# Two transformer blocks on one core: squares of the first norm between the conditioning slabs, norm roots by logarithm and exponential, low parts on VectorE, weights split late

## What is computed

```python
def rms_norm(x, g, eps):
    return x * lax.rsqrt(jnp.mean(x * x, -1, keepdims=True) + eps) * g

mod = silu(c) @ w_ada[l] + b_ada[l]            # shift, scale, gate, two times
a_x = rms_norm(h_x, g_mix[l]) * (1 + sc1) + sh1   # norm mix, tokens
a_c = rms_norm(h_c, g_mix[l]) * (1 + csc1) + csh1 # the same for the context rows
y_x, y_c = mixer(a_x, a_c, w_in[l], ...)       # projections, a Fourier mix, two attentions
h_x = h_x + gt1 * y_x
f_x = rms_norm(h_x, g_ffn[l]) * (1 + sc2) + sh2   # norm ffn
h_x = h_x + gt2 * conv_ffn(f_x, ...)
```

## Time and profile before

| what | us |
|---|---|
| runs (3) | 2770.31, 2776.19, 2776.48 |
| median | 2776.19 |
| profiled execution, its own time | 2759.57 |
| its span, first to last instruction | 2757.8 |
| TensorE matmul busy | 2562.5 (93%) |
| VectorE busy | 1576.3 (57%) |
| ScalarE busy | 1219.8 (44%) |
| POOL busy | 187.4 (7%) |
| mean granted TensorE clock | 0.974 |

### The profile page before, as it was taken

The page is one execution under the profiler, slowest core; times in us unless marked ns, Lnnn a source line. Parts: engine busy times, 40 slices in busy tenths (PEclk is TensorE's granted clock), DMA queues, the critical chain, the costliest instruction groups (busy, mean ns, idle before and its releaser), DMA issues.

```text
span 2757.8 us, 42208 instructions
## 1 busy us (share of the span) xinstructions
PE 2562.5 (93%) x17840; PEld 2259.0 (82%) x17840; DVE 1576.3 (57%) x2657; ACT 1219.8 (44%) x2025; POOL 187.4 (7%) x239
## 2 busy tenths in 40 slices
PE   5997899998999998999989989999799999988999
PEld 2875577776777776878889989998799999976999
DVE  2333234545565555364668877666566675766665
ACT  3224334424333324354556554445444553555543
POOL 0000000000000000000000011010010110025100
PEclk8998999999999999999999999999899999999999
DMA  7224432231454543233354546554265456530554
GB/s 243 67 86 131 134 105 84 67 99 61 136 169 138 168 131 129 85 115 101 122 168 155 190 145 207 185 168 130 71 201 190 153 191 199 168 126 16 169 197 140
DMA packets 337387, 382.12 MB, mean 139 GB/s; under 512 B 7408, under 2 KB 301296, under 8 KB 337200
## 3 DMA queue, kind: packets, MB, share of 16 engines
q1 hardware_dynamic: 334656, 370.37, 41.2%
q0 software_dynamic: 2544, 9.06, 1.1%
HBM read 378.36 MB, written 1.05 MB: 138 GB/s over the span
## 4 chain that ended last, share of the span: by engine, by line
PE 77%; DVE 10%; ACT 8%; DMA 3%; issue 2%; POOL 0%; SPq 0%; DVEq 0%; ACTq 0%; POOLq 0%
PE PS L1207 20%; PE PS L1209 19%; PE PS L1208 19%; DVE WL L1899 3%; ACT WH L1579 2%; PE PS L1242 1%; PE PS L1244 1%; PE PS L1243 1%; PE PS L1255 1%; PE PS L1224 1%; DMA RAWB<-in_w_in 1%; PE PS L1225 1%; PE PS L1226 1%; PE PS L1273 1%; PE PS L1340 1%
## 5 line engine op out<-in xcount | busy, mean ns | idle before, releaser
L1899 DVE TENSOR_TENSOR WL<-RAWB,WH 128x1024 fp32r<-128x1024 f32 (+2 forms) x613 | 734.7, 1206 | 650.5 <-ACT WH L1579 649.0
L1207 PE MATMUL PS<-AH,WH 128*128 128x256 f32 (+1 forms) x2912 | 910.7, 313 | 13.8 <-DVE WL L1899 13.8
L1209 PE MATMUL PS<-AH,WL 128*128 128x256 f32 (+1 forms) x2912 | 896.6, 308 | 0.0
L1208 PE MATMUL PS<-AL,WH 128*128 128x256 f32 (+1 forms) x2912 | 896.5, 308 | 0.0
L1579 ACT ACTIVATE WH<-RAWB 128x1024 fp32r<-128x1024 f32 (+2 forms) x613 | 625.3, 1033 | 320.0 <-PE PS L1209 167.1
L1207 PEld LDWEIGHTS PS<-AH,WH 128*128 128x128 f32 x2912 | 548.9, 189 | 70.1 <-issue 22.1
L1209 PEld LDWEIGHTS PS<-AH,WL 128*128 128x128 f32 x2912 | 548.7, 188 | 31.1
L1208 PEld LDWEIGHTS PS<-AL,WH 128*128 128x128 f32 x2912 | 548.5, 188 | 29.6 <-issue 0.5
L1207 PE MATMUL PS<-BH,WH 128*128 128x256 f32 (+1 forms) x1440 | 452.2, 314 | 0.8 <-DVE WL L1899 0.8
L1209 PE MATMUL PS<-BH,WL 128*128 128x256 f32 (+1 forms) x1440 | 439.2, 305 | 0.0
L1208 PE MATMUL PS<-BL,WH 128*128 128x256 f32 (+1 forms) x1440 | 438.5, 305 | 0.0
(11 more groups left out here) (314 smaller groups left out, 2827.9 us busy)
## 6 DMA issues: line engine op xcount, KB each, us to landing
RAWB<-in_f_in SPq DMA_DIRECT2D x88, 1024.0 KB, 5.2
RAWB<-in_w_in SPq DMA_DIRECT2D x52, 1024.0 KB, 5.1
RAWB<-in_w_ada SPq DMA_DIRECT2D x48, 1024.0 KB, 5.4
RAWB<-in_w_up SPq DMA_DIRECT2D x44, 1024.0 KB, 5.2
RAWB<-in_f_out SPq DMA_DIRECT2D x40, 1024.0 KB, 5.1
RAWB<-in_w_down SPq DMA_DIRECT2D x20, 1024.0 KB, 5.3
RAWB<-in_sb_qkv SPq DMA_DIRECT2D x12, 1024.0 KB, 5.4
RAWB<-in_w_out SPq DMA_DIRECT2D x8, 1024.0 KB, 5.1
```

The source lines that it names most:

```text
L1207: pe.matmul(out, h, xh[:, 0:T], start=k == 0, stop=False)
L1208: pe.matmul(out, h, xl[:, 0:T], start=False, stop=False)
L1209: i = pe.matmul(out, l, xh[:, 0:T], start=False, stop=k == g.kt - 1)
L1899: dve.tensor_tensor(c.part("WL", p), c.raw(p.slab)[:, k0:k1, c0:c1], c.part("WH", p).bitcast(F32), ALU.subtract).then_inc(up("lo", ("lo", ...
```

## The change

Six edits. (1) The eight squares and sums of the norm `mix0` are put into the list one behind each of the eight yields of `ada(0, 0, 16)`, that is one per conditioning slab; the last sum and then splits of two pieces follow. (2) The root of a `NormPlan` norm is the exponential of minus half the logarithm, both on ScalarE; the reciprocal is gone. The early table load is an explicit load of set 6, which line 1790 also loads. (3) All low parts of tiles are made by VectorE. (4) `split` lets `ahead` fill the ring of four pieces only up to two before the tiles, up to three behind the sixth tile, and fully at the end. (5) The lead waits for a piece's high part before its first matmul on it, and for its low part before the third. (6) `consts1` is loaded when slab 5 has been used.

```diff
-    def ahead(self):
-        while self.next_piece < len(self.pieces) and not self.held[self.next_piece % NW]:
+    def ahead(self, most=NW):
+        while sum(self.held) < most and self.next_piece < len(self.pieces) and not self.held[self.next_piece % NW]:
...
-        self.finish(self.ada(0, 0, 16))
-        nrm = self.layer(0, NormPlan(self, "mix0", 512, ("side", "ctxT")))
+        nrm = NormPlan(self, "mix0", 512)
+        for k, _ in enumerate(self.ada(0, 0, 16)):
+            nrm.add(k, ("side", "ctxT"))
+        nrm.sum()
+        self.ahead(2)
+        self.flush()
+        nrm = self.layer(0, nrm)
...
         plan.mark("A" + name)
-        plan.ahead()
+        plan.ahead(2)
...
             if k > 1:
                 low[k - 2]()
+            if k == 5:
+                plan.ahead(3)
         low[6]()
         low[7]()
+        plan.ahead()
...
+                if name == "consts1":
+                    on.wait_ge(*at("used_raw", 5))
...
-        elif s.kind == "nlow" and s.n % 2:
-            W, a0 = s.x
-            on.wait_ge(*at("xhi", s.id[0], s.n))
-            pool.tensor_tensor(AL[:, s.n, a0:a0 + W], c.tmp(s.t)[:, 0:W], AH[:, s.n, a0:a0 + W].bitcast(F32),
-                               ALU.subtract).then_inc(up("xlo_pool", ("xlo", s.id[0], s.n)), 1)
...
-            for p in s.p:
-                on.wait_ge(*at("lo", p.p))
...
+                    if k == 0:
+                        on.wait_ge(*at("hi", p.p))
                     pe.matmul(out[j], h, xh[:, 0:T], start=k == 0, stop=False)
                     pe.matmul(out[j], h, xl[:, 0:T], start=False, stop=False)
+                    if k == 0:
+                        on.wait_ge(*at("lo", p.p))
...
-                on.wait_ge(*at("eps"))
-                act.activation(EPS[:, 2:3], EPS[:, 0:1], ACT.Sqrt)
+                act.add_instruction(mybir.InstLoadActFuncSet(name=nc.get_next_instruction_name(), act_func_set_id=6, ins=[], outs=[]))
...
-            act.activation(RS[:, 0:s.n], c.bank(s.b)[:, 0:s.n], ACT.Sqrt, bias=EPS[:, 0:1], scale=1.0 / 1024).then_inc(
+            on.wait_ge(*at("eps"))
+            r = RS[:, 0:s.n]
+            act.activation(r, c.bank(s.b)[:, 0:s.n], ACT.Ln, bias=EPS[:, 0:1], scale=1.0 / 1024).then_inc(
                 up("acted", ("sd", id[0])), 1)
+            on.wait_ge(*at("sd", id[0]))
+            act.activation(r, r, ACT.Exp, scale=-0.5).then_inc(up("acted", ("rs", id[0])), 1)
...
-        elif kind == "rstd":
-            on.wait_ge(*at("sd", id[0]))
-            dve.reciprocal(RS[:, 0:s.n], RS[:, 0:s.n]).then_inc(up("vec", ("rs", id[0])), 1)
...
-        elif kind == "nlow" and s.n % 2 == 0:
+        elif kind == "nlow":
```

More of the change, by code:

```diff
@@ L876, with __init__ @@
 class NormPlan:
-    def __init__(self, plan, name, T, at_once=None):
+    def __init__(self, plan, name, T):
         self.plan, self.name, self.T, self.b, self.n, self.square = plan, name, T, None, 0, None
-        if at_once:
-            for k in range(8):
-                self.add(k, at_once)
     def add(self, k, after):
@@ L2365, in build @@
         mem["banks"] = [ctx.enter_context(nc.psum_tensor(f"PS{i}", [128, 512], F32)) for i in range(8)]
-        mem["sem"] = {n: sem(n) for n in ("acc", "hi", "acted", "lo", "vec", "xlo_pool", "sums", "rooted", "pooled")}
+        mem["sem"] = {n: sem(n) for n in ("acc", "hi", "acted", "lo", "vec", "sums", "rooted", "pooled")}
         mem["rawsem"] = [sem(f"raw{i}") for i in range(NR)]
```

## The result

The median of 11 runs was 2752.91 us, against 2771.68 us for the kernel before in the same comparison (11 runs). The ratio is 0.9932, with a 95% interval of 0.9920 to 0.9945: 18.8 us faster (15.2 to 22.2), where 25.5 us were forecast. The profiled execution took 2750.89 us (span 2749.1 us) at a mean granted clock of 0.977 (before 2759.57, 2757.8 and 0.974).

The account below looks back on a forecast made before the run. TensorE was taken as the bound (77% of the chain), with gains where it stands still: opening 13.2, ffn0 3.8, mix1 4.5, ffn1 2.4, leads 1.6, together 25.5 us off 2776.2, so 2751 us; range 2740 to 2766.

Parts of the forecast that it names:

- Part 1: Opening: squares and sums moved between slabs, last sum ending at 42.0 us instead of 51.28, a gain of 9.3 us.
- mixed clock: Opening: TensorE's first 6 us at the low clock level, the rest high.
- rival A: Opening: TensorE stays at the low clock level, so the opening gains 2.0 us; 2762 us in all, chance 0.16.
- cost nothing: Opening: tables loaded behind slab 5 are first read after the projection, so no cost; uncovered, 1.3 us each.
- Part 2: Norms' root: reciprocal replaced by an exponential, saving 2.7 us at three norms and 1.3 at ffn1.
- part 3: Weight splits late: with the new root 3.9 us gained in the opening; 1.08 us more at each later norm.
- part 4: Odd tiles' low parts on VectorE instead of POOL: shows only where the last tile ends the lead, 0.67 us at mix1.
- the lead's 48 matmuls ... and the piece after it cover them: Held-back splits: ScalarE's 1 us and VectorE's 1.1 each hidden by at least 10 us of lead; uncovered, 2.1 us each.
- a stop inside a lead on a late piece: Listed sign that the forecast is wrong: TensorE stopping within a lead for a held-back weight piece.
- Part 5: Finer waits in the leads: 1.1 us at 1984.88 and 0.5 at one more, together 1.6; bounds 0 and 6.6.
- Rival E: Slower: late splits free raw buffers late, slabs 39.7 us late in all, uncovered by TensorE; 2790 us, chance 0.04.
- Rival B: Everything at the high clock: opening 1.8 us more, leads 2 us more at three norms; 2743 us, chance 0.13.

Follow-up runs that it names:

- e6: e5 plus the opening's turned conditioning rows copied into the tiles' buffers instead of the squares'; 2749.70 us, 0.9923 of the kernel before.
- e9: e6 with consts1 held until slab 7 has been used instead of slab 5; 2750.77 us, 0.9910 of the kernel before.
- e7: Changed kernel with odd tiles' low parts on POOL again; 2753.87 us, 0.9935 of the kernel before.
- e4: Changed kernel with splits as far as the ring goes, ahead of the tiles, again; 2754.58 us, 0.9949 of the kernel before.
- e3: Changed kernel with square root on ScalarE and reciprocal on VectorE again at the norms; 2759.60 us, 0.9961 of the kernel before.
- e8: Changed kernel with the lead's first matmul waiting for both pieces' low parts again; 2751.66 us, 0.9917 of the kernel before.
- e2: Changed kernel with the first norm's eight squares and sums behind all eight slabs again; 2762.78 us, 0.9969 of the kernel before.
- e12: The kernel before run again, no edit, for a second trace; 2770.79 us, 0.9990 of the kernel before.
- e10: Changed kernel with consts1 loaded at the start again, not held back; 2753.95 us, 0.9927 of the kernel before.
- e5: Changed kernel with the opening's third piece split behind all eight tiles, not behind the sixth; 2746.53 us, 0.9904 of the kernel before.
- e11: The same kernel as e5 in a second comparison; 2751.84 us, 0.9921 of the kernel before.
- e1: The changed kernel run again, no edit; 2749.61 us, 0.9931 of the kernel before.

## Why the prediction was right, and where it was off

**The time and the gain.** The time came out at 2752.91 for 2751, but the gain at 18.8 for 25.5. The forecast was taken off a median of three runs, 2776.19; eleven runs of the same kernel gave 2771.68, and 25.5 less than that is 2746.2. So 4.5 us of the close hit are luck, and what is to be explained is a gain 6.7 us short.

**Part 1** held. 9.3 us forecast; the last sum ended 9.5 us earlier (51.28 to 41.79), 9.6 between the two repeats (52.72 to 43.10). The mixed clock that I took for the opening (the first part low, the rest high) is what the rows show; rival A would have had the last sum at 53. One clause is true of this kernel only: that the tables loaded behind slab 5 "cost nothing". Here TensorE's own list hides them. In e6, without the waits for the row copies, slab 7 starts 1.8 us later than in e9, and the first projection matmul 4.6 us later (53.28 and 48.70).

**Part 2 and the norms of part 3** held in their sum. Idle time before the leads fell by 3.56 us at ffn0 (3.8 forecast), 3.71 at mix1 (3.8, with 0.9 more from part 4 where 0.7 was forecast; part 4 had not counted that VectorE's products get faster too, as e7 shows), 2.17 at ffn1 (2.4) and 3.75 in the opening (3.9). That they add up is partly owed to their being made together, which my working did not see. From the four idle times at each norm (before, e4, e3, after):

| norm | before | new root, early splits (e4) | old root, late splits (e3) | both |
|---|---|---|---|---|
| ffn0 | 8.45 | 6.96 | 7.61 | 4.89 |
| ffn1 | 5.36 | 5.26 | 4.52 | 3.19 |

At ffn1 the new root with early splits brings 0.10 us: nearly all of the 1.33 that it saves it gives back, since a copy that was hidden by the reciprocal comes to stand behind the exponential. Once no copy is due ahead of the tiles, all of it counts.

**The step that failed in part 3** is "the lead's 48 matmuls ... and the piece after it cover them". I took the third piece's 1 us and 1.1 us as filling of idle engines and did not ask what stands behind them in VectorE's order. In the opening two tiles do, and the piece's two halves lie on two engines, the slower of which comes last. The price was 1.98 and 2.75 us, near the 2.1 that the prediction gives as the uncovered price. It also listed "a stop inside a lead on a late piece" among the signs of being wrong. Only the opening paid it: at ffn0 and mix1 three pieces were held already and nothing was due at the sixth tile.

**Part 5** was sized at 1.6 us, of which 1.1 at the lead near 1985. That lead gained more: 1.8 to 2.9 us in nine of the eleven traces with the edit and 0.6 in the other two, counted from the end of the lead before it. Elsewhere the working took a moved stop for a shortened one: near 1629 the lead ends no sooner. From the end of ffn1's lead to the end of the last nothing is left of it: 1126.7 and 1133.6 us in the two changed traces, 1130.8 in e8, 1124.6 and 1128.0 before. Its worth in the total is not shown.

**Rival E** did not come: the stage behind ffn1, with its late splits, is as long as it was (195.8 us to the end of the next lead, 195.6 before), and each norm brought a gain. **Rival B** did not come as a whole: the opening's first sum took 2.05 us at the low level, and ffn0's lead still opens with 0.76 us for its first matmul. A little of it shows at ffn1, where the lead took 7.1 and 7.9 us against 8.3 and 8.4 before.

**What is not settled** is where the rest of the 25.5 us is. The stop in the opening's lead accounts for 2 us of it. In the traces 21.0 us are there at the end of ffn1's lead, 17.2 at the end of the last lead, and 10.4 at the end; the last stage alone lost 6.8 us without having been edited. The timed runs have no traces, so I can't say how often they had the long or the short last stage. Two things speak against taking the 6.8 us as the price of the change in every execution. Both traced executions of before were quick ones (2759.57 and 2769.41, where the medians of before lay between 2770.7 and 2773.9 in the four comparisons), so the traces understate the gain. And e2's trace has the short last stage, but its ratio is 10.5 us behind the changed kernel's, as much as its opening lost and not 7 us less, though with some 6 us of noise in that difference. Neither is proof: for the last stage alone no kernel has shown both lengths.

## What to carry to other kernels

When a step with a half on each of two engines is put off into a stream of other work, look at the engine that runs ahead: it waits in order for the half of the engine that lags, and holds back all that is queued behind. Put such a step where the streams end. And cost an operation that moves to another engine by what that engine did meanwhile: the same exponential was worth 1.5 us or 2.7 us at the same norm, depending on whether a copy was hidden by the reciprocal it replaced. A wait that is only made finer inside a lead brings nothing when the last thing awaited is the same, unless the clock stays up with it, as at one lead here (1.00 and 0.83 against 0.65).

## What the runs showed of the hardware

At a granted clock of 1.00, matmuls of 256 columns issued back to back come at one of two spacings, 113.3 or 117.8 ns, and keep to it for tens to hundreds of microseconds. Twenty microseconds of the last stage by engine (columns PE, PEld, DVE, ACT, POOL, granted clock, DMA share, GB/s), changed kernel and then e12:

```profile
2600.00:2620.00 20.00, 20.00 (x172) 20.00 (x171) 12.57 (x19) 10.42 (x16) 2.96 (x4) 1.00 0.63 207
```

```profile
2600.00:2620.00 20.00, 20.00 (x179) 20.00 (x179) 14.45 (x25) 11.10 (x18) 2.39 (x4) 1.00 0.56 181
```

TensorE is without a gap in both, the clock is full in both, and 179 matmuls pass in one where 172 pass in the other: 4%. In the last stage both traces of the kernel before, e2 and e10 had the short spacing (182.6 to 183.0 us) and the other ten traces of the changed family the long one (189.2 to 189.7 us). In other stages one and the same kernel shows both in different executions. The clearest pair is e5 and e11, the same kernel (us, PE busy, clock, DMA share, GB/s):

```profile
1520.00:1540.00 20.00, 20.00 (x179) 1.00 0.69 229
```

```profile
1520.00:1540.00 20.00, 20.00 (x172) 1.00 0.63 206
```

Near 2230 us it is the changed kernel (117.8) and e1 (113.3). So in those stages it isn't the program alone. In the last stage it may be: neither the squares between the slabs (e10 has them) nor the early consts1 (e2 has not) decides it by itself, but each kernel that was traced twice gave the same length twice. I found no cause.
